# One streaming-encoder layer on one core: how semaphores are given back between the stages

## What is computed

```python
h = rms_norm(x, g_pre_mix)
u_a, v_a, q, k, v_b = split(h @ w_in)                       # 1024 -> 5 * 1024
y_a = gelu(u_a) * (tril(w_s) @ layer_norm(gelu(v_a)) + b_s) # per group and 128 positions
y_b = stick_breaking(q, [past_k, k], [past_v, v_b])         # 16 heads of 64
g_a, g_b = split(sigmoid(h @ w_gate + b_gate))
merged = g_a * (y_a @ w_branch_a) + g_b * (y_b @ w_branch_b)
x = x + rms_norm(merged @ w_o, g_post_mix)
up = rms_norm(x, g_pre_ffn) @ w_up                          # 1024 -> 5632
gate, val = split(causal_conv3(up))
x = x + rms_norm((gelu(gate) * val) @ w_down, g_post_ffn)
```

## Time and profile before

| | us |
|---|---|
| median of 3 runs (2263.41 to 2264.87) | 2264.02 |
| the profiled execution, its device time | 2264.9 |
| its span, first to last instruction | 2262.9 |
| busy in the span: PE / PE weight loads | 2162.2 / 2051.3 |
| busy: DVE / POOL / ACT | 1276.1 / 865.6 / 756.1 |
| mean granted TensorE clock, of full speed | 0.985 |

### The profile page before, as it was taken

One profiled execution on the slowest core, in us unless ns is written; L12 is line 12 of the kernel. 1 busy time (PEld: TensorE's weight loads), 2 busy tenths in 40 slices (PEclk: granted clock), 3 DMA queues, 4 the chain that ended last, 5 costly groups with the idle time before them and its releaser, 6 DMA issues. The chain is left out here.

```text
span 2262.9 us, 33667 instructions
## 1 busy us (share of the span) xinstructions
PE 2162.2 (96%) x12884; PEld 2051.3 (91%) x12884; DVE 1276.1 (56%) x1730; ACT 756.1 (33%) x1450; POOL 865.6 (38%) x494
## 2 busy tenths in 40 slices
PE   6999999998999899997999989999999999999996
PEld 6999999997899899997999978889999999999995
DVE  5045120002787777847656557476767667676756
ACT  4222111223666667753342123212121211112124
POOL 2335333444655555547564210143232232323213
PEclk9999999999999999998999999999999999999998
DMA  5125424546554455554666432221111111101104
GB/s 175 47 68 186 130 78 117 162 141 169 147 128 123 120 123 131 139 162 131 180 185 196 152 112 93 66 65 56 34 50 37 46 44 40 53 30 56 34 13 169
DMA packets 286602, 236.95 MB, mean 105 GB/s; under 512 B 48966, under 2 KB 262678, under 8 KB 286486
## 3 DMA queue, kind: packets, MB, share of 16 engines
q1 hardware_dynamic: 277744, 221.72, 33.9%
q10 hardware_dynamic: 7510, 9.19, 1.2%
q0 software_dynamic: 1232, 4.46, 0.5%
HBM read 168.25 MB, written 67.07 MB: 104 GB/s over the span
## 5 line engine op out<-in xcount | busy, mean ns | idle before, releaser
L170 PE MATMUL ps_up<-mergedT_lo,p_w_hi 128*128 128x364 f32 x1056 | 347.0, 329 | 3.4 <-ACT p_up_gate L2354 2.9
L172 PE MATMUL ps_up<-mergedT_hi,p_w_lo 128*128 128x364 f32 x1056 | 347.8, 329 | 0.0
L171 PE MATMUL ps_up<-mergedT_hi,p_w_hi 128*128 128x364 f32 x1056 | 347.4, 329 | 0.0
L291 PE MATMUL p_psB<-hT_lo,w_hi 128*128 128x364 f32 x888 | 295.9, 333 | 2.4 <-issue 2.4
L291 PE MATMUL p_psB<-hT_hi,w_lo 128*128 128x364 f32 x888 | 293.4, 330 | 0.0
L291 PE MATMUL p_psB<-hT_hi,w_hi 128*128 128x364 f32 x888 | 292.7, 330 | 0.0
L1145 DVE TENSOR_TENSOR_SCAN p_rest<-p_rest 128x896 f32<-128x896 f32 (+7 forms) x128 | 226.4, 1780 | 91.5 <-ACT p_rest L1078 91.2
L2393 DVE TENSOR_TENSOR p_acc<-p_psD,p_acc 128x512 f32<-128x512 f32 x360 | 247.7, 690 | 40.4 <-PE p_psD L172 39.1
L150 POOL TENSOR_SCALAR p_w_hi<-p_w_raw 128x1024 fp32r<-128x1024 f32 x64 | 68.1, 1065 | 518.5 <-PE p_psD L172 397.6
L936 POOL TENSOR_TENSOR p_weights<-p_weights,p_rest 128x895 f32<-128x895 f32 (+7 forms) x128 | 170.4, 1341 | 190.7 <-DVE p_rest L1145 190.7
L170 PEld LDWEIGHTS ps_up<-mergedT_lo,p_w_hi 128*128 128x128 f32 x1056 | 199.1, 189 | 5.8 <-ACT p_up_gate L2354 3.2
(11 more groups left out here) (331 smaller groups left out, 4680.7 us busy)
## 6 DMA issues: line engine op xcount, KB each, us to landing
p_w_raw<-in_w_up SPq DMA_DIRECT2D x44, 512.0 KB, 3.7
w_raw<-in_w_in SPq DMA_DIRECT2D x40, 512.0 KB, 4.0
p_w_raw<-in_w_down SPq DMA_DIRECT2D x22, 512.0 KB, 3.5
p_kT<-k_hi_scratch SPq DMA_DIRECT2D x32, 256.0 KB, 4.9
p_kT<-k_lo_scratch SPq DMA_DIRECT2D x32, 256.0 KB, 5.4
w_raw<-in_w_gate SPq DMA_DIRECT2D x16, 512.0 KB, 4.1
p_raw_v<-in_cache_sb_v SPq DMA_DIRECT2D x8, 1024.0 KB, 6.1
p_raw_k<-in_cache_sb_k SPq DMA_DIRECT2D x7, 1024.0 KB, 6.4
```

Source lines behind the costliest of these rows:

```text
L170: nc.tensor.matmul(out, stat_hi, mov_lo, start=first, stop=False)
L171: nc.tensor.matmul(out, stat_hi, mov_hi, start=False, stop=False)
L172: return nc.tensor.matmul(out, stat_lo, mov_hi, start=False, stop=last)
L291: last = nc.tensor.matmul(out[:, 0:CH], stat[:, slot, w], mov[:, k, c], start=(at == 0), stop=(at == 3 * KT - 1))
```

## The change

Every stage gets its semaphores by number from one of two fixed banks, in turn; those that cross borders all come from a third. Nothing is cleared at a border and the second barrier is gone. POOL clears the bank of the stage before, as the first instruction of the next stage, with one range. At the end of the program POOL clears all three banks with one range, and no barrier follows it. `early` is merged into `kept`. One call of `sem_clear` issues one EVENT_SEMAPHORE_RANGE_CLEAR and no DRAIN.

```diff
+ODD, EVEN, KEPT = range(256 - 70, 256), range(256 - 118, 256 - 70), range(256 - 157, 256 - 118)
 class Sems:
-    def __init__(self, nc, stack, phase):
+    def __init__(self, nc, stack, phase, numbers):
         self.nc, self.phase, self.known = nc, phase, {}
+        self.free = iter(numbers)
         stack.callback(self.give_back)
     def give_back(self):
-        self.nc.clear_and_free_semaphores(list(self.known.values()))
-        self.nc.all_engine_barrier()
+        for sem in self.known.values():
+            self.nc.release_semaphore(sem)
     def __call__(self, name):
         if name not in self.known:
-            self.known[name] = self.nc.alloc_semaphore(f"{self.phase}_{name}")
+            self.known[name] = self.nc.alloc_semaphore(f"{self.phase}_{name}", num=next(self.free))
         return self.known[name]
...
-        kept = Sems(nc, whole, "kept")
+        kept = Sems(nc, whole, "kept", KEPT)
...
-            early = Sems(nc, both, "early")
...
+        nc.gpsimd.sem_clear(range(KEPT.start, 256))
...
-        s = Sems(nc, ctx, "p1")
+        s = Sems(nc, ctx, "p1", ODD)
...
-        s = Sems(nc, ctx, "p4")
+        s = Sems(nc, ctx, "p4", EVEN)
...
             @block.gpsimd
             def _(pool):
+                pool.sem_clear(ODD)
                 def weigh(b):
...
```

More of the change, by code:

```diff
@@ L275, in build_layer @@
         with ExitStack() as both:
-            early = Sems(nc, both, "early")
             ps_up = both.enter_context(nc.psum_tensor("ps_up", [P, 4, 512], F32))
-            phase_output(nc, a, ident, mgT, d.x2, ffn_ring, o_raw, kept, early, ps_up, r0, region, rf, f_size)
-            phase_ffn(nc, a, o, ident, par, mgT, d.x2, ffn_ring, early, ps_up, ffn_place.at, r0, region, rf, f_size)
+            phase_output(nc, a, ident, mgT, d.x2, ffn_ring, o_raw, kept, ps_up, r0, region, rf, f_size)
+            phase_ffn(nc, a, o, ident, par, mgT, d.x2, ffn_ring, kept, ps_up, ffn_place.at, r0, region, rf, f_size)
+        nc.gpsimd.sem_clear(range(KEPT.start, 256))
 def feature_part(nc, out, ring, slot, pair, chunk, first=0, count=3 * KT):
@@ L1253, in phase_sample_attention @@
     with ExitStack() as ctx:
-        s = Sems(nc, ctx, "p3")
+        s = Sems(nc, ctx, "p3", ODD)
         f = Place(nc, start, size)
@@ L1420, in _ @@
             def _(pool):
+                pool.sem_clear(EVEN)
                 def split_w(n):
@@ L1778, in phase_merge @@
     with ExitStack() as ctx:
-        s = Sems(nc, ctx, "p6")
+        s = Sems(nc, ctx, "p6", EVEN)
         f = Place(nc, start, size)
@@ L1873, in _, with phase_output @@
                 lo(len(ORDER) - 1)
-def phase_output(nc, a, ident, mgT, x2_dram, ffn_ring, w_raw, kept, early, ps_up, r0, r0_size, rf, rf_size):
+def phase_output(nc, a, ident, mgT, x2_dram, ffn_ring, w_raw, kept, ps_up, r0, r0_size, rf, rf_size):
     w_o = a["w_o"][0].rearrange("(k p) c -> p k c", p=P)
@@ L1886, in phase_output @@
     with ExitStack() as ctx:
-        s = Sems(nc, ctx, "p7")
+        s = Sems(nc, ctx, "p7", ODD)
         AHEAD, SLOT_BYTES = Weights.AHEAD, SLOT * 4
@@ L1933, in _ @@
                     sp.dma_start(next_raw[:, n, :].rearrange("p (k c) -> p k c", k=KT),
-                                 w_up[:, :, P:2 * P] if n else w_down).then_inc(early(f"raw_ahead{n}"), 16)
+                                 w_up[:, :, P:2 * P] if n else w_down).then_inc(kept(f"raw_ahead{n}"), 16)
             @block.gpsimd
             def _(pool):
+                pool.sem_clear(EVEN)
                 for n in range(AHEAD):
@@ L1990, in up @@
                                             h2T[0][:, k, cols], h2T[1][:, k, cols], k == 0, k == KT - 1)
-                    last.then_inc(early("up_opened"), 1)
+                    last.then_inc(kept("up_opened"), 1)
                 product(0)
@@ L2082, in _, with phase_ffn @@
                     lo(m)
-def phase_ffn(nc, a, o, ident, par, h2T, x2_dram, ffn_ring, early, ps_up, ffn_ring_end, r0, r0_size, rf, rf_size):
+def phase_ffn(nc, a, o, ident, par, h2T, x2_dram, ffn_ring, kept, ps_up, ffn_ring_end, r0, r0_size, rf, rf_size):
     w_up = a["w_up"][0].rearrange("(k p) c -> p k c", p=P)
@@ L2100, in phase_ffn @@
     with ExitStack() as ctx:
-        s = Sems(nc, ctx, "p8")
+        s = Sems(nc, ctx, "p8", EVEN)
         f_ = Place(nc, ffn_ring_end, rf + rf_size - ffn_ring_end)
@@ L2157, in _ @@
                 for n in range(AHEAD):
-                    sp.wait_ge(early(f"raw_ahead{n}"), 16)
+                    sp.wait_ge(kept(f"raw_ahead{n}"), 16)
                     sp.sem_inc(ring.raw_ready[n], 16)
@@ L2220, in step @@
                     if first:
-                        pe.wait_ge(early("up_opened"), UP_EARLY)
+                        pe.wait_ge(kept("up_opened"), UP_EARLY)
                         pe.sem_inc(s("up"), UP_EARLY)
```

## The result

| | before | after |
|---|---|---|
| median device time, us | 2264.28 (2262.47 to 2265.05, 6 runs) | 2254.57 (2245.83 to 2255.18, 6 runs) |
| ratio, 95% interval | | 0.995 (0.994 to 0.996) |
| profiled execution: device time / span, us | 2264.9 / 2262.9 | 2250.26 / 2248.1 |

The kernel became faster by 9.7 us; 12.9 were forecast. The range, 2248.5 to 2257.0, holds the median. The profiled execution is one of the faster ones. The first view is the page: its span, and the busy times.

The account below looks back on a forecast made before the run. TensorE bounds the kernel, busy 2162.2 of 2262.9 us. Borders 6.3, clock 3.2 and end 3.4 us sum to 12.9 us, giving 2251.1 us from the 2264.02 median; range 2248.5 to 2257 us.

Parts of the forecast that it names:

- First border, 0: Border after prompt attention: SP's loads still wait for the last stores to land, so 0 gained, 0.1 us at most.
- Third and fifth border with the clock, 1.9 + 1.5 and 1.6 + 1.7: Borders ending merge and ffn: stages move forward 1.9 and 1.6 us; half-clock stretches behind them vanish, worth 1.5 and 1.7.
- The clears inside stages, 0: Five range clears on POOL at stage starts: 0.4 or 0.3 us each, covered by slack, so no cost.
- The end, 3.4: Program end: 4.3 us of clears and barriers become one 157-number clear of 0.9 us, gaining 3.4 us.
- Rival D: Wide clears at the end and inside stages are slow, making the kernel slower: 2269.5 us; chance 0.02.
- the upper price in B: Program end: the wide clear costs 6.9 us, so the end loses 2.6 us: 2257.1 us.
- Rival C: Borders: the clears covered fetching the next stage's code, so borders and clock give nothing: 2260.6 us; chance 0.04.
- Second border, 1.2: Border ending sample attention: everything the next stage needs is issued after the release, so it moves forward 1.2 us.
- Fourth border, 1.6: Border ending the output stage: the DVE split chain PE waits for starts at the release, so 1.6 us gained.
- rival A: Clock not won back: half-clock stretches stay or others come in their place, 2252.8 to 2256.0 us; chance 0.20.
- The 2 us outside the span: Device time beyond the span: left unchanged in the forecast; a rival had it grow as engines stop apart.
- rival B: End gives less: the wide clear takes its upper price, or time outside the span grows; chance 0.06.

Follow-up runs that it names:

- the kernel with VectorE first: Changed kernel, with GpSimd's multiply at the first pair of heads in sample attention waiting until VectorE's is done: 2248.52 us, ratio 0.9931.
- the long end: Changed kernel with an end like the one before: 21 clears, each behind a DRAIN, and three barriers, in place of one range clear: 2256.05 us, ratio 0.9964.

## Why the prediction was right, and where it was not

The sign, the range and most terms held. Medians of the span say how much. On the one occasion with spans of both kernels it fell from 2262.2 to 2251.6 us, that is by 10.6, where 12.9 were forecast, and the device time by 9.7. (The median spans of the kernel before in other sets of runs were 2261.0 to 2262.4, so each such difference is good to about 1 us.) The terms that were off all gave less than forecast, so none hid another in the medians. In the profiled pair it is otherwise: its spans differ by 14.8 us, more than forecast, because sample attention gave 5.5.

**First border, 0: right.** Stage lengths of the four traces with the old border had a mean of 467.8 us (467.2 to 468.7), those of the nine with the new one 467.7 (466.8 to 468.6), so a gain of some tenths would not show. SP waits at L893 as the step said, and its first load leaves 1.7 us after the release. The scores came at 537.03, 11.3 us behind the release as before (11.5), not sooner. PE's 0.54 us became 3.39, more than the "some 2" of the text, but it is idle time that was waiting for the same load. The clock that the step feared for did fall, at 535.56 for 10.2 us, where the kernel before had it low at 527.0 and at 540.66 for 3.4 us each; the stage is no longer for it.

**Third and fifth border with the clock, 1.9 + 1.5 and 1.6 + 1.7: right.** Merge took 97.8 to 98.0 us in the three traces with the old borders and no wait added and 94.6 or 94.7 in every one with the changed borders; ffn 807.1 to 807.2 and 804.0 to 804.2. That is 3.3 and 3.1 us against 3.4 and 3.3.

**The clears inside stages, 0: right.** 0.42 and 0.29 us against 0.4 and 0.3. With the clear at the end of GpSimd's program instead of the start, sample attention took 223.2 against 223.1, both with VectorE first.

**The end, 3.4: right in the span.** 0.9 us remained, and 5.5 ns a number from two narrow rows gave the wide one within 2%: 902 ns for 157 numbers, 887 measured. Rival D and the upper price in B are out. Rival C is out too: PE resumed 0.26 us behind its release. The trace of the kernel before also answers C's open question, whether the engines branch at a border: of its 48 branch instructions none comes before 1440.2 us and none between that one and 1501.0, so none lies at any of the five.

**Second border, 1.2: the step failed.** "Everything that this stage needs is issued after the release, so the whole stage moves forward" took the stage to have one length. It has two, by which of two multiplies starts first, 0.1 to 0.6 us apart, and these are 3 to 6 us apart in the unforced traces, 5.6 when forced. In the slower group, to which the three unforced traces with the old borders belong (228.6 to 228.9), the stage fell only to 228.1 to 228.3: 0.3 to 0.8 us of the 1.2. Why not all of it, I did not follow to the end; PE works at 1.2 GHz behind both of its waits there, and the second of these stretches is 6.8 or 10.2 us long in that group, 3.4 or 6.8 in the other, and differs from trace to trace. The profiled execution hit the faster group and showed 5.5, which one trace would have credited to the change.

**Fourth border, 1.6: sometimes.** Of the nine traces with the changed borders five have 130.1 to 130.3 us for the output stage, against 132.0, and so the 1.6 and a little more. In the other four it took 131.3 to 131.6, with a half-clock stretch that begins about 122 us behind the release (1433 in the profiled execution, 12 matmuls in 3.41 us, above). That is rival A in part: not the old stretches that stay, but a new one behind pauses of 1.01 and 0.52 us, which PE makes in every trace, in a stage where the text had counted no clock. It costs some 1.3 us. The changed borders are not what makes it: it also came in one of the four traces with the old ones (133.3 us against 132.0).

**"The 2 us outside the span": the other step that failed.** It stood in rival B with 0.06, and the forecast left it unchanged. In 6 of 11 executions of the changed kernel it was 3.0 to 3.2 us, and in 5 it was 1.8 to 2.2. That is 0.6 to 1.0 us on the median. The text had looked for covered fetches at the borders (rival C) and not at the end, where the one fetch lay. The Trainium skill, "Runtime: NRT & Kernel Launch", section "Instruction fetch mechanics", calls the crossing of a 16 KiB boundary "mostly hidden". At the borders these traces agree: behind the second release of the changed kernel a packet of 16 KB begins on q8 at 995.06 and takes 1.43 us, while PE, which had resumed at 994.06, 0.26 us after the release, works on. At the end of the program it was not hidden in about half of the executions, by some 1.1 us (by 1.9 in one of the kernel with VectorE first, 4.02 us).

The shortfall of 3.2 us is 2.3 in the span (12.9 - 10.6) and 0.9 outside it. By parts it adds up to about 0.7 in sample attention, nothing to 1.2 in the output stage, 0.6 to 1.0 outside the span and 0.3 in merge and ffn: 1.6 to 3.2. That the fetch behind the last instruction is what lengthens those executions rests on two things: the packet and the long rest go together in ten traces out of ten, and the long end removes both. No run moved the packet alone, so it is strongly supported and not shown; why it lies there in some executions only, and whose code it is, stays open. So does what makes the clock fall in the output stage in some executions.

## What to carry to other kernels

Give semaphores back with as few clears as possible: neighbouring numbers in one range, inside the next stage, out of two banks in turn; at the borders the range clear is most of the gain (4.6 of 6.6 us) and the second barrier the smaller part. Where one stage's length comes out 5 us different from trace to trace, compare the first place where two engines start side by side, and fix the order by a wait if one order is better; a profile of one execution cannot give such a difference to an edit. Judge a shortened end by the device time, not by the span: what was covered by the tail may come to lie behind it.

## What was not expected of the hardware

**VectorE and GpSimd slow each other, and the order matters.** A multiply of 128 x 1024 took VectorE 1.22 to 1.26 us in four traces in which it began first (1.37 and 1.72 in two more), and 2.76 to 3.11 when GpSimd's of 128 x 1087 was under way; 3.42 when it waited for that one and ran beside GpSimd's next work. GpSimd's took 2.1 us when it began first and 3.0 to 3.1 when second. At the second pair of heads, where the two do not overlap, they took 1.22 and 2.11. So it is mostly the one that comes second that is slowed.

**A range clear costs by the number.** 44 ns for one number, 67 to 71 for 7 or 8, 138 for 18, 285 to 289 for 48, 413 to 420 for 70 and 887 for 157: over the whole range 5.4 ns for each further one. A barrier of all engines behind it cost 0.3 us.

**The clock does not follow PE's last pause alone.** At the third border it fell to 1.2 GHz after a pause of 2.37 us in the kernel before and stayed at 2.4 after one of 2.37 in the same kernel with VectorE first. In the output stage it fell behind pauses of 1.01 and 0.52 us in four of nine traces and stayed behind the same two in five. It fell there in one of four traces with the old borders too. A term for it in a sum is a chance, not a sure gain or loss.
